# Layer 0's modulation vectors made in four places of the program, and filler matmuls in three norms

## The reference

```python
mod = (c_act @ w_mod[l] + b_mod[l])[:, None, :]
modc = cc_act @ w_mod[l] + b_mod[l]
sh1, sc1, g1, sh2, sc2, g2 = jnp.split(mod, 6, axis=-1)
px = (rmsnorm(x, norm1_g[l]) * (1.0 + sc1) + sh1) @ w_in[l] + b_in[l]
...
x = x + g1 * (y_x @ w_out[l])
x = x + g2 * swiglu(rmsnorm(x, norm2_g[l]) * (1.0 + sc2) + sh2, w_gu[l], w_down[l])
```

## Time and profile before

| | |
|---|---|
| median of 3 runs | 2835.37 us (2829.86 to 2836.59) |
| profiled execution, its time | 2841.22 us |
| profiled execution, its span | 2839.2 us |
| PE busy | 2642.4 us (93%) |
| DVE busy | 1594.3 us (56%) |
| POOL busy | 1362.3 us (48%) |
| ACT busy | 761.0 us (27%) |
| chain that ended last | PE 75%, DVE 13%, ACT 4%, issue 3%, POOL 2%, DMA 2% |
| DMA | 256.53 MB, mean 90 GB/s; 378 GB/s in the first fortieth of the span |

### The profile page before, as it was taken

The page is one execution under the profiler, slowest core; times in us unless marked ns, Lnnn a source line. Parts: engine busy times, 40 slices in busy tenths (PEclk is TensorE's granted clock), DMA queues, the critical chain, the costliest instruction groups (busy, mean ns, idle before and its releaser), DMA issues.

```text
span 2839.2 us, 38165 instructions
## 1 busy us (share of the span) xinstructions
PE 2642.4 (93%) x14172; PEld 2177.7 (77%) x14172; DVE 1594.3 (56%) x2160; ACT 761.0 (27%) x1565; POOL 1362.3 (48%) x1014
## 2 busy tenths in 40 slices
PE   7698999799999997999889999899999999888988
PEld 7587887688888885788667878678888887666776
DVE  7897254674573766815443333445555555656855
ACT  1222444311111123134421111312222222233423
POOL 2233223355455443333457667565555554544454
PEclk9999999899999998999999999899999999999999
DMA  9211012233232321111123232333333322223221
GB/s 378 99 53 45 30 38 104 75 124 120 89 121 94 119 84 60 53 52 53 59 69 95 93 93 91 101 106 97 95 91 97 92 89 88 82 66 90 79 93 60
DMA packets 78393, 256.53 MB, mean 90 GB/s; under 512 B 9776, under 2 KB 13616, under 8 KB 77744
## 3 DMA queue, kind: packets, MB, share of 16 engines
q1 hardware_dynamic: 60416, 211.64, 22.6%
q10 hardware_dynamic: 17840, 43.03, 4.8%
HBM read 237.33 MB, written 2.10 MB: 84 GB/s over the span
## 4 chain that ended last, share of the span: by engine, by line
PE 75%; DVE 13%; ACT 4%; issue 3%; POOL 2%; DMA 2%; ACTq 0%; SPq 0%; DVEq 0%; POOLq 0%
PE PS L405 19%; PE PS L408 18%; PE PS L406 18%; PE PS L1427 3%; PE PS L1428 3%; PE PS L1429 3%; DVE AC L2140 3%; DVE cprod L2112 2%; PE PS L616 1%; PE PS L627 1%; POOL w_lo L399 1%; DMA modv<-in_wmod 1%; PE PS L1414 1%; DVE Z L2083 1%; PE PS L611 1%
## 5 line engine op out<-in xcount | busy, mean ns | idle before, releaser
L399 POOL TENSOR_TENSOR w_lo<-raw,w_hi 128x1024 fp32r<-128x1024 f32 (+1 forms) x331 | 879.6, 2657 | 27.6
L405 PE MATMUL PS<-XH,w_hi 128*128 128x512 f32 x2168 | 825.1, 381 | 51.5 <-DVE XL L2090 11.9
L406 PE MATMUL PS<-XL,w_hi 128*128 128x512 f32 x2168 | 797.1, 376 | 0.0
L394 POOL TENSOR_TENSOR word<-ones 128x1 f32<-128x1 f32 x331 | 107.1, 323 | 1396.7 <-PE PS L408 974.5
L408 PE MATMUL PS<-XH,w_lo 128*128 128x512 f32 x2168 | 747.2, 376 | 0.0
L405 PEld LDWEIGHTS PS<-XH,w_hi 128*128 128x128 f32 x2168 | 412.6, 190 | 165.8 <-issue 37.0
L406 PEld LDWEIGHTS PS<-XL,w_hi 128*128 128x128 f32 x2168 | 412.7, 190 | 75.1
L408 PEld LDWEIGHTS PS<-XH,w_lo 128*128 128x128 f32 x2168 | 382.8, 190 | 60.1
L397 POOL TENSOR_SCALAR w_hi<-raw 128x1024 fp32r<-128x1024 f32 (+1 forms) x331 | 354.8, 1072 | 0.0
L2112 DVE CUSTOM_DVE_ANT_0 cprod<-modv,cb 128x1024 f32<-128x1024 f32 x152 | 259.5, 1707 | 26.7 <-DMA modv<-in_wmod 21.6
L1427 PE MATMUL PS<-XH,w_hi 128*128 128x512 f32 (+1 forms) x640 | 236.8, 370 | 37.7 <-DVE XL L2090 37.7
(11 more groups left out here) (311 smaller groups left out, 3477.5 us busy)
## 6 DMA issues: line engine op xcount, KB each, us to landing
raw<-in_wgu SPq DMA_DIRECT2D x88, 512.0 KB, 3.4
raw<-in_wa SPq DMA_DIRECT2D x80, 512.0 KB, 3.5
raw<-in_win SPq DMA_DIRECT2D x48, 512.0 KB, 3.5
modv<-in_wmod ACTq DMA_DIRECT2D x48, 512.0 KB, 4.9
raw<-in_wdn SPq DMA_DIRECT2D x32, 512.0 KB, 3.6
modv<-in_wmod SPq DMA_DIRECT2D x28, 512.0 KB, 11.2
QS<-Z ACTq DMA_DIRECT2D x100, 128.0 KB, 3.3
modp<-in_wmod SPq DMA_DIRECT2D x20, 512.0 KB, 12.1
```

Of the source, the lines that this page charges most:

```text
L394: pool.tensor_tensor(word[:, 0:1], ones[:, 0:1], ones[:, 0:1], ALU.mult)
L399: pool.tensor_tensor(lo, src, hi.bitcast(FP32), ALU.subtract).then_inc(s_split, 1)
L405: pe.matmul(acc(s)[:, a:b], hi, rh[:, i, a:b], start=i == 0, stop=False)
L406: pe.matmul(acc(s)[:, a:b], hi, rl[:, i, a:b], start=False, stop=False)
```

## The change

For layer 0 the 48 tiles of the modulation are no longer made together.

- Tiles 0 to 7 (sh1): PE. The weights come as rows, PE transposes each in 8 pieces (`mod_row_transposed`), ACT copies them out of PSUM, PE sums them (`mod_row_sum`).
- Tiles 8 to 15 (sc1): DVE at the head (`mod_row`).
- Tiles 16 to 23 (g1): DVE in the input projection (`late_rows`), three before `gated_linear(0)` and five after it.
- Tiles 24 to 27: POOL multiplies (8 products of 1024 values, after the split of tile 1) and ACT sums (8 instructions after the norm, before the evacuation of tile 0).
- Tiles 28 to 47: PE with matmuls of 2 columns (`mod_sum`): 28 to 31 after the first norm's sum, 32 to 35 after tile 12 of the input projection, 36 to 38 before and 39 to 41 after the sum of norm 1, 42 to 45 between the feature tiles of `first_tiles`, 46 and 47 after it.
- `X` comes in 8 parts between the rows. The remaining constants come later in SP's stream, and PE waits for them in front of the input projection.
- `keep_running`: 4 matmuls of ones on ones, 512 columns wide, whose result nobody reads, before the sum of norms 2, 3 and 4, and after it 6 (norm 2) or 4 (norms 3 and 4).
- In layer 1 the first four weight tiles of `w_in` are loaded before SP waits for the end of layer 0, and ACT waits for `s_mod` after the reciprocal root and not before it.

The core of the diff:

```diff
+        def keep_running(pe, n):
+            for _ in range(n):
+                pe.matmul(PS[:, 4, :].rearrange("p (a c) -> p a c", c=P), ones[:],
+                          ones[:].rearrange("p (a c) -> p a c", a=1).to_broadcast([P, 4, P]), start=True, stop=True)
...
             for i in range(k0, min(k1, last)):
+                if between:
+                    between(i)
                 pe.wait_ge(sem, done + i + 1)
...
+            for k in range(KT):
+                sp.dma_start(rowp[k][:], wmod_d[0, k]).then_inc(s_modw[k], 16)
+                sp.dma_start(X[:, k], xT[:, k]).then_inc(s_xp[k], 16)
+                sp.dma_start(rowd[k][:], wmod_d[0, KT + k]).then_inc(s_mvw[k], 16)
...
                 if l:
+                    for p in range(RING):
+                        load(n0 + p, win_d[l, IN_ORDER[p]])
                     sp.wait_ge(s_tile, n0)
                     sp.wait_ge(s_used, used(n0 - 1))
+                else:
+                    for p in range(2):
+                        load(n0 + p, win_d[l, IN_ORDER[p]])
+                sp.dma_start(wg[:], wg_d[l]).then_inc(s_par, 16)
+                if l == 0:
+                    for i in range(4):
+                        sp.wait_ge(s_mvd, i + 1)
+                        sp.wait_ge(s_modd, i + 1)
+                        mod_chunk(T_FIRST + i, s_modw[i])
+                    for i in range(4):
+                        sp.dma_start(rowq[i][:], wmod_d[0, 3 * KT + i]).then_inc(s_prow, 16)
+                    for j in range(3):
+                        late_row(j)
...
                         sp.wait_ge(s_htr, NJ)
                         sp.dma_start(X[:], xT).then_inc(s_x, 16)
+                        for m in range(36, MODS):
+                            if m == 45:
+                                sp.wait_ge(s_y, KT)
+                            mod_chunk(m, s_modw[m - 36])
...
+            def mod_products():
+                pool.wait_ge(s_mvd, KT)
+                pool.wait_ge(s_prow, 16 * 4)
+                for i in range(4):
+                    for n in range(2):
+                        pool.tensor_tensor((prod, rowq)[n][i][:], rowq[i][:], cb[:, n, :], ALU.mult).then_inc(s_mvp, 1)
...
             def norm(q, w):
+                for m in (36, 37, 38) if q == 1 else ():
+                    mod_sum(m, 5, 2 * (m - 36))
+                if q > 1:
+                    keep_running(pe, 4)
                 pe.wait_ge(s_acc, KT * (q + 1))
...
                 last.then_inc(s_squ, 1)
+                if q > 1:
+                    keep_running(pe, 6 if w == T else 4)
...
-                    pe.wait_ge(s_cact, 1)
-                    for m in range(MODS - MOD_V):
...
+                    mod_row_transposed(0)
+                    for k in range(1, KT):
+                        mod_row_transposed(k)
+                        mod_row_sum(k - 1)
+                    mod_row_sum(KT - 1)
                 norm(2 * l, T)
+                if l == 0:
+                    for i in range(4):
+                        mod_sum(T_FIRST + i, 4, 2 * i)
+                    pe.wait_ge(s_const, 16 * 4)
...
+                if l == 0:
+                    for i in range(4):
+                        for n in range(2):
+                            act.wait_ge(s_mvp, 2 * i + n + 1)
+                            v = (prod, rowq)[n][i][:]
+                            last = act.activation(v, v, ACT.Identity, scale=0.5, accum_out=mods[0][:, 3 * KT + i, n:n + 1])
...
+                if l == 0:
+                    mod_read(T_FIRST, T_FIRST + 4, 4, KT + 4).then_inc(s_modr, 1)
+                    dve.wait_ge(s_const, 16 * 4)
+                    late_rows(0, 3)
...
                 gated_linear(0)
+                if l == 0:
+                    late_rows(3, KT)
                 convolve(l, w, cuts[0], cuts[1])
...
+                if l == 0:
+                    mod_read(T_FIRST + 4, T_FIRST + 8, 3, KT + 8).then_inc(s_modr, 1)
                 convolve(l, w, cuts[4], cuts[5])
```

More of the change, by code:

```diff
@@ L43 @@
 MOD_V = 28
-MOD_P = 8
+MOD_D = 16
+T_FIRST = 28
 GA_T, U_T, SV_T, K_T, V_T, Q_T, O_T = 0, 4, 6, 8, 12, 16, 20
@@ L300, in build_program @@
         s_x = sem("x_loaded")
+        s_xp = [sem(f"x_feature_tile_loaded{k}") for k in range(KT)]
+        s_c = sem("c_loaded")
+        s_id = sem("identity_loaded")
+        s_pcl = sem("columns_of_parameters_loaded")
+        s_prow = sem("mod_rows_for_pool_loaded")
+        s_mvp = sem("mod_products_made")
+        s_mva = sem("mod_products_summed")
+        s_mtr = sem("mod_rows_transposed")
+        s_mev = sem("mod_rows_transposed_evacuated")
+        s_modr = sem("mod_sums_read")
         s_par = sem("layer_parameters_loaded")
@@ L1254, in _ @@
-                for p in range(N_IN):
+                    sp.dma_start(tri[:].rearrange("p a b -> p (a b)"), consts_d[:, P:3 * P]).then_inc(s_const, 16)
+                    sp.dma_start(mskd[:].rearrange("p a b -> p (a b)"), consts_d[:, 3 * P:5 * P]).then_inc(s_const, 16)
+                    sp.dma_start(dsel[:], consts_d[0:8, 5 * P:5 * P + 2]).then_inc(s_const, 16)
+                    sp.dma_start(fin_g[:], fin_d).then_inc(s_const, 16)
+                for p in range(RING if l else 2, N_IN):
+                    if l == 0 and p in (4, 5):
+                        if p == 4:
+                            sp.wait_ge(s_xn, KT)
+                            for i in range(4):
+                                mod_chunk(T_FIRST + 4 + i, s_modw[4 + i])
+                        for j in ((3, 4, 5), (6, 7))[p - 4]:
+                            late_row(j)
@@ L1315, in norm, with mod_sum, mod_row_transposed, mod_row_sum @@
                 last.then_inc(s_squ, 1)
+                if q > 1:
+                    keep_running(pe, 6 if w == T else 4)
+            def mod_sum(m, bank, col):
+                i = m - T_FIRST
+                pe.wait_ge(s_modw[i if i < KT else i - KT], 32 if i < KT else 48 if i < 2 * KT else 16)
+                for k in range(KT):
+                    last = pe.matmul(PS[:, bank, col:col + 2], modt[m][:, k, :], cact[:, k, :], start=k == 0, stop=k == KT - 1)
+                last.then_inc(s_modd, 1)
+            def mod_row_transposed(k):
+                pe.wait_ge(s_modw[k], 16)
+                if k >= 2:
+                    pe.wait_ge(s_mev, k - 1)
+                for i in range(KT):
+                    last = pe.transpose(banks(2 * (k % 2), 2 * (k % 2) + 2)[:, i * P:(i + 1) * P], rowp[k][:, i * P:(i + 1) * P], ident[:])
+                last.then_inc(s_mtr, 1)
+            def mod_row_sum(k):
+                pe.wait_ge(s_mev, k + 1)
+                if k == 0:
+                    pe.wait_ge(s_cact, 1)
+                for i in range(KT):
+                    last = pe.matmul(PS[:, 5, 2 * k:2 * k + 2], rowt[k % 2][:, i, :], cact[:, i, :], start=i == 0, stop=i == KT - 1)
+                last.then_inc(s_modd, 1)
             def transpose_tile(l, e, src, nj):
@@ L2116, in mod_tiles @@
                     last.then_inc(s_mvd, 1)
-                    dve.wait_ge(s_mvd, (MOD_V if l else 0) + first + u + 1 + dyn)
+                    dve.wait_ge(s_mvd, MOD_D + first + u + 1 + dyn)
                 at = bass.ds(first + dyn, 4)
@@ L2159, in _ @@
             activate_c(0)
-            for g in range(MOD_V // 4):
-                mod_tiles(0, 4 * g, 0, 4 * (g % 2), g // 2 + 1, link)
+            for k in range(KT):
+                mod_row(rowd[k], (s_mvw[k], 16), KT + k, k)
             for l in range(DEPTH):
```

187 lines of the change are left out of this document (121 added, 66 removed).

## The result

The changed kernel takes 2817.8 us (median of 5 runs, 2817.1 to 2826.05), the kernel before 2835.37 (5 runs beside them): 0.9941 of it, 95% interval 0.9926 to 0.9956. That is 17.6 us faster, where 5.0 were forecast. The profiled executions are 23.4 us apart, 2841.22 and 2817.8 us. A second measurement on another chip gave 0.9951 [0.9936, 0.9966].

A forecast was written before the change was run, and what follows sets the result against it. At the head PE only sums modulation tiles under saturated DMA; DVE paces the input projection. -43.7 + 21.1 + 2.0 + 10.2 + 2.0 + 15 - 11.6 = -5.0 us, forecast 2830.4 us, range 2812 to 2847.

The forecast's parts named there:

- Head, -43.7: Work up to tile 0 of the input projection: done at 88 us in place of 131.7, gaining 43.7 us.
- E: Moment when tile 0 of the input projection is done: 131.68 us before the change, forecast at 88.
- `lf`, +21.1: Input projection: DVE's added work makes `lf` late, PE waits about 20 us, 21.1 us of the gain given back.
- Slow restart, +2.0: Input projection: after standing 20 us for `lf`, PE restarts slowly, costing 2.0 us.
- Tiles 32 to 35, +10.2: Input projection: DVE stands while PE sums these four tiles, the clock holding about 3 us; costs 10.2 us.
- it shows again in the wait for `Ug`, which stays as long as it was: Input projection: the cost of tiles 32 to 35 shows again at PE's wait for `Ug`, 7.5 us before and unchanged.
- `X` behind 12 tiles, +2: Reload of `X`: 12 modulation tiles ahead of output tile 4's weights delay these, costing 2 us (0 to 6).
- Norm 1, +15: Sums of tiles 36 to 47 around norm 1, partly at low clock, delay PE's restart by 15 us.
- the low clock holds to k = 5: Rival: low clock lasts from norm 1 to feature-tile step k = 5; norm 1 costs 30, 2845 us; chance 0.18.
- Norms 2 to 4, -11.6: Norms 2 to 4: fillers keep the clock up and norm 2's scalings run without splits; gains 11.6 us together.
- the clock stays up: Rival: high clock during sums; tiles 32 to 35 cost 6.9, norm 1 costs 6; 2818 us; chance 0.29.

The follow-up runs named there:

- ones at the head: Changed kernel plus a 384-column matmul of ones ahead of every block of transposes and every sum at the head; 0.9939 of the kernel before.
- Half the products: Changed kernel with POOL's eight products and ACT's eight sums of them taking 512 of 1024 values; 0.9933 of the kernel before.
- The short sums: Changed kernel with the sums of tiles 32 to 35 doing only the first of their eight products each; 0.9916 of the kernel before.
- the second profile: The changed kernel run once more, unaltered, beside three follow-up runs; 2823.5 us, 0.9951 of the kernel before.
- the sums in the wait for `lf`: Changed kernel with the sums of tiles 32 to 35 moved directly ahead of PE's wait for `lf`; 2810.14 us, 0.9912 of the kernel before.

## Why the prediction was right or wrong, step by step

- **Head, -43.7:** right, -43.2, and for the reasons given: rows every 5.0 us (5.1 forecast), scaling at 55.8 (59), products of POOL over DVE's norm. In one thing I had it only half: PE set the start of the norm, but DVE and POOL set its end, and with the low clock taken away (ones at the head) E gains 1.1 us. Half the products give 4.0.
- **`lf`, +21.1:** too much; E to `lf` grew by 15.6 us (23.7 to 39.3). The mechanism is right (15.7 us of wait, the longest), the size is not. The first three rows (10.55 us from 84.19 on, beside one split) and `gated_linear(0)` (4.54, beside the other) take 15.1 us together, where I had 7.6 + 5.8 + 1.9 = 15.3: that part was right. But the rows begin 4.2 us ahead of E, where I had 2.0 (86 and 88). The trace of before already has 4.2 us from the end of DVE's norm to E, and 85 and 88 leave 3: that is most of these 2.2 us. The five later rows took 15.5 (16.6), and the 12 taps behind them 8.3 in place of 10.3, since no split lay beside them: I had kept a duration of before with its own collision in it.
- **Slow restart, +2.0:** 2.4.
- **Tiles 32 to 35, +10.2:** the four sums were 9.42 us, the products behind them slow. But the step "it shows again in the wait for `Ug`, which stays as long as it was" failed. That wait fell from 7.5 to 2.5: DVE's stand took in the split that had slowed the taps (2.8 us), and PE's slow products cost nothing, as DVE is late there anyhow. Of the 9.0 us lost up to the first `sgu_mix`, 2.5 come back by DVE and 2.7 because the clock no longer falls behind the wait for `Ug`. Net 3.8 us. The short sums show the counterpart: `Ug` is back at 7.3, the products behind it at 2.83, and 3.9 us come back in place of 7.5.
- **`X` behind 12 tiles, +2:** 1.4 us from the log weights to the output products and 1.6 more until norm 1, 3.0 in all; in the second profile 0.8 in all. No run tests this term by itself.
- **Norm 1, +15:** 13.0 in this profile, with each part where it was forecast. In three of nine profiles the low clock lasts 6 us longer. The rival "the low clock holds to k = 5" was no alternative to the forecast but one of two courses that the same kernel takes; it got as far as k = 2.
- **Norms 2 to 4, -11.6:** -5.5, -2.5 and -2.9, together -10.9. The ones do what was forecast of them, 6.4 us of 6.6.
- **Not priced:** the profile is ahead by another 6.8 us, in places where the change moves none of PE's work: 3.6 in layer 1's projection, 1.2 in the FFN ahead of norm 4, 2.0 behind norm 4. The two that I followed up are waits of 2 us (`lf`, and `HL` in the FFN ahead of norm 4) behind which the clock fell in one execution and not in another. The second profile of the changed kernel is ahead of the kernel before by 16.4 us, not 23.3.
- **The rival "the clock stays up" is refuted**, though its 2818 was the time: 3.4 us a tile in the head, 10.24 for three tiles at norm 1, and the windows there (columns: stretch, length, busy time of PE, PEld, DVE, ACT and POOL with their counts, granted clock, DMA) show half clock while PE is never idle:

```profile
495.00:500.00 5.00, 5.00 (x17) 3.79 (x17) 0.00 (x0) 1.06 (x2) 0.00 (x0) 0.50 0.00 0
500.00:505.00 5.00, 5.00 (x25) 5.00 (x25) 2.54 (x6) 2.96 (x4) 0.00 (x0) 0.50 0.00 2
515.00:520.00 5.00, 5.00 (x37) 4.61 (x36) 4.87 (x10) 2.25 (x4) 0.00 (x0) 1.00 0.02 3
```

0.50 is 1.2 GHz. The Trainium skill (TensorE: Matmul & The Clock Gate, What's actually happening) has activity release the throttle; at 500 to 505 PE is busy without a pause and the clock stays at half, so for matmuls of two columns this trace does not bear the sentence out.

So the 12.6 us between forecast and result are `lf` (5.5), `Ug` (6.4) and norm 1 (2.0), less 2.6 of small things of the other sign (head, restart, `X`, norms 2 to 4), and what is left is within the scatter of the executions. All three are sizes read too high. Of the first two, 2.0 and 2.5 us have one cause, a collision of POOL with DVE counted where it no longer fell; 2.2 at `lf` are a start of DVE's rows put too late against E, and 2.7 at `Ug` the slow products behind a wait that had become short. That the time came out at 2817.8, nearer to the refuted rival's 2818 than to the 2830.4, is thus no sign for that rival.

## What to carry to other kernels

Where two engines exclude each other, an operation's duration in the trace contains its neighbour's work: strip that out before moving the operation, and ask at the new place what it will collide with. A wait is only the place where a busy engine is noticed: taking five rows of DVE's work from ahead of one consumer, `lf`, which then came 12.6 us earlier, moved the wait to three others, while moving PE's work into the wait, and taps to behind `Ug`, brought 13 us in the profile at the output products (8.3 at its end) and 12 to 17 in the medians, by which of the two measurements of the changed kernel it is set against. A longer wait can also cost more than itself, by the clock behind it: compare the products behind it too. And a profile of one execution carries luck in the clock, here some 6 us at one norm; compare events of several profiles before explaining the last few microseconds.

## What the runs showed of the hardware that I had not expected

- In the head of the changed kernel, transposes and sums of two columns that follow each other without a pause from 16.19 to 66 us ran at the low clock (3.41 us for a tile). With a matmul of 384 columns (0.8 to 0.9 us) ahead of each block of eight transposes and of each sum, the head ran at 2.4 GHz from the second row's transposes on (1.84 us for a tile). Where only one such matmul came per sum, the clock fell at the third sum (tiles 28 to 31: 1.84, 1.84, 2.96, 3.41 us) or at the second (norm 1).
- The same wait of 2.0 us costs nothing or 1.5 to 3 us, by whether the clock falls behind it; the changed kernel showed both in two executions.
- After the sums 39 to 41 the clock came back within one step of products (3.8 us) in six profiles and only behind the third step in three, with the same instructions around the norm. In one of the six (the sums in the wait for `lf`) it had been up during a part of these sums already, 7.13 us in place of 10.24.
- A POOL product takes 2.34 us alone and 2.5 to 2.8 beside DVE, while DVE's four scalings go from 2.2 to 8.5: DVE bears most of the collision.
